# A prompt and sample decoder step on one core: sample attention dealt out inside the heads' loop, HBM tables cleared behind the cached values, first stage reordered

## What is computed

```python
def run_trunk(x, q_pos0, past_rows, past_win, ...):
    # layer 0: gMLP mixer, then dense SwiGLU (1024 -> 2816 -> 1024)
    z = gelu(rmsnorm(x) @ w_in);  u, v = split(z)
    v = layernorm(v, ln_g, ln_b)                       # the first stage of the kernel
    x = x + (u * (causal(W_s) @ v + b_s)) @ w_out
    x = x + swiglu(rmsnorm(x))
    # shared keys and values: compression, selection, window (4 groups of 64)
    kv = rmsnorm(x) @ w_kv                             # plus, for samples, cached pages and a window
    kc, vc = compress_blocks(...)                      # MLP over 32-row blocks, stride 16
    # layer 1: attention of 16 heads over three branches, ALiBi, sigmoid gates
    o = g0 * softmax(q kc) vc + g1 * softmax(q ks) vs + g2 * softmax(q kw) vw
    x = x + o @ w_out
    x = x + moe(rmsnorm(x))                            # top 2 of 8 SwiGLU experts
    return rmsnorm(x), kv rows, window, normed v
```

## Time and profile before

| | |
|---|---|
| Runs | 1326.03 us median, 1325.71 to 1331.93 |
| Profiled execution | 1325.86 us, its span 1324.3 us |
| TensorE busy | 1248.7 us (94%) |
| VectorE busy | 1042.1 us (79%) |
| ScalarE busy | 927.7 us (70%) |
| GpSimd busy | 76.4 us (6%) |
| Mean granted clock of TensorE | 0.977 of full speed |

### The profile page before, as it was taken

How to read it: one execution, slowest core, us unless ns; L and a number is a source line. 1 busy time by engine, 2 the same in 40 slices (tenths; PEclk the granted TensorE clock), 3 DMA queues, 4 the chain that set the end, 5 groups by cost and what they waited for, 6 DMA issues and landing times.

```text
span 1324.3 us, 21438 instructions
## 1 busy us (share of the span) xinstructions
PE 1248.7 (94%) x7272; PEld 1063.9 (80%) x7272; DVE 1042.1 (79%) x1463; ACT 927.7 (70%) x1378; POOL 76.4 (6%) x77
## 2 busy tenths in 40 slices
PE   6889999999996879999999999999999999999996
PEld 6879999999964668788788888888888888887874
DVE  6767666567523965898998998998998998989985
ACT  5555444456462895787987987987888888878863
POOL 1000000004210000200000000000000000003400
PEclk9999999999996889899999999999999999999998
DMA  8374455557589108699998998998998998998930
GB/s 342 129 252 172 183 191 192 191 191 254 160 318 418 61 4 347 266 423 393 357 416 333 388 413 322 406 406 319 413 402 324 415 392 333 416 380 326 410 133 33
DMA packets 59711, 391.50 MB, mean 296 GB/s; under 512 B 6686, under 2 KB 12962, under 8 KB 21186
## 3 DMA queue, kind: packets, MB, share of 16 engines
q1 hardware_dynamic: 51010, 354.29, 68.0%
q0 software_dynamic: 8640, 36.40, 7.4%
HBM read 367.41 MB, written 27.45 MB: 298 GB/s over the span
## 4 chain that ended last, share of the span: by engine, by line
PE 73%; DVE 10%; ACT 7%; issue 5%; SPq 3%; DMA 2%; DVEq 0%; ACTq 0%
PE bank L1838 16%; PE bank L1840 16%; PE bank L1839 16%; PE bank L1469 7%; PE bank L1470 7%; PE bank L1471 7%; DVE w_lo L1351 3%; ACT arena L756 2%; SPq L429 2%; DMA win_v_past<-in_win_v 2%; DVE d_lo L969 1%; PE bank L1823 1%; ACT slc_v L763 1%; ACT d_hi L604 1%; ACT w_hi L831 1%
## 5 line engine op out<-in xcount | busy, mean ns | idle before, releaser
L1351 DVE TENSOR_TENSOR w_lo<-raw,w_hi 128x1024 fp32r<-128x1024 f32 x528 | 622.7, 1218 | 36.0 <-ACT w_hi L831 18.4
L831 ACT CAST w_hi<-raw 128x1024 fp32r<-128x1024 f32 x528 | 543.2, 1056 | 93.3 <-PE bank L1840 92.3
L1838 PE MATMUL bank<-w_hi,xg_hi 128*128 128x512 f32 x704 | 275.0, 391 | 1.5 <-DVE w_lo L1351 1.5
L1840 PE MATMUL bank<-w_hi,xg_lo 128*128 128x512 f32 x704 | 274.4, 390 | 0.0
L1839 PE MATMUL bank<-w_lo,xg_hi 128*128 128x512 f32 x704 | 274.0, 389 | 0.0
L969 DVE TENSOR_TENSOR d_lo<-ring,d_hi 128x1024 fp32r<-128x1024 f32 x120 | 146.0, 1223 | 92.4 <-ACT d_hi L604 92.3
L1469 PE MATMUL bank<-hA_hi,d_hi 128*128 128x264 f32 x640 | 185.9, 291 | 18.4 <-DVE hA_lo L959 9.1
L1470 PE MATMUL bank<-hA_lo,d_hi 128*128 128x264 f32 x640 | 183.2, 286 | 0.0
L1471 PE MATMUL bank<-hA_hi,d_lo 128*128 128x264 f32 x640 | 182.9, 286 | 0.0
L604 ACT CAST d_hi<-ring 128x1024 fp32r<-128x1024 f32 x120 | 124.8, 1043 | 66.9 <-PE bank L1471 60.0
L1838 PEld LDWEIGHTS bank<-w_hi,xg_hi 128*128 128x128 f32 x704 | 132.1, 188 | 29.3 <-DVE w_lo L1351 2.2
(11 more groups left out here) (311 smaller groups left out, 1485.1 us busy)
## 6 DMA issues: line engine op xcount, KB each, us to landing
raw<-in_moe SPq DMA_DIRECT2D x264, 1024.0 KB, 6.7
ring<-in_wd SPq DMA_DIRECT2D x29, 2048.0 KB, 8.4
out_rows<-zeros POOLq DMA_DIRECT2D x1, 6656.0 KB, 60.3
slot_rows<-zeros POOLq DMA_DIRECT2D x1, 6144.0 KB, 30.3
out_rows<-yrow POOLq DMA_DIRECT2D x8, 512.0 KB, 7.0
xs<-slot_rows POOLq DMA_DIRECT2D x7, 512.0 KB, 3.6
arena<-in_cmp_pages POOLq DMA_DIRECT2D x16, 128.0 KB, 3.3
X2v<-in_cmp_pages POOLq DMA_DIRECT2D x16, 128.0 KB, 2.6
```

What stands on the lines that cost most here:

```text
L831: nc.scalar.copy(w_hi[:, i % NSPLIT, :], raw[:, u % NRAW, ITEM * (i % 2):ITEM * (i % 2) + ITEM])\
L1351: V.tensor_tensor(w_lo[:, i % NSPLIT, :], raw[:, (i // 2) % NRAW, ITEM * (i % 2):ITEM * (i % 2) + ITEM], w_hi[:, i % NSPLIT, :].bitcast(F3 ...
L1838: T.matmul(out, lhs_hi, hi, start=first, stop=False)
L1840: return T.matmul(out, lhs_lo, hi, start=False, stop=last)
```

## The change

1. **First stage.** ScalarE rounds, and VectorE makes the remainder of, one item more before each gelu and behind each scaling (`round_to("vu", c + 1)`, `rest_to("vu", k + 1)`). The u scalings and the items are spread over the layer norm at other places.
2. **Third transpose group.** It goes to the bank STAT, without the wait for VectorE's copy.
3. **Sample scores** go to STAT and MISC instead of B[0] to B[2]; their exponentials `Ss` and the turned weights `PTs` lie in `X2v`, no longer in a buffer of the heads' scores.
4. **Sample attention** is cut into blocks (`sample_max`, `sample_scale`, `sample_turned`, `sample_out` on VectorE; `sample_turn`, `sample_values`, `sample_sum` on TensorE) that stand between the blocks of pairs 0 to 3. `scores(0)` no longer waits for the sample maxima, and `scores(1)` no longer stands behind the value product.
5. **Clears.** GpSimd waits for all cached values (`past_v_in`) before it issues them.

```diff
@@ gpsimd
             pool.wait_ge(zeros_ready, 1)
+            pool.wait_ge(past_v_in, 16 * (NS * PAGES + 1))
             for rows in (slot_rows.rearrange("b p n -> (b p n)"), out_rows[0:NO_ROW, :].rearrange("r n -> (r n)")):
@@ scalar
             for c in range(KC):
-                round_to("vu", c)
+                round_to("vu", c + 1)
                 act.wait_ge(v_scaled, c + 1)
...
             for c in range(KC):
-                round_to("vu", KC + c)
+                round_to("vu", KC + c + 1)
...
             exp_head(0)
             exp_head(1)
+            exp_head(2)
+            exp_head(3)
             act.wait_ge(orow_done, 1)
             nc.scalar.copy(orow[:, :], MISC[:, :]).then_inc(orow_ready, 1)
-            exp_head(2)
-            exp_head(3)
@@ vector
             for k in range(KC):
-                rest_to("vu", k)
                 scaled(vT[:, k, :], "vu", k, v_scaled)
+                rest_to("vu", k + 1)
                 if k:
                     add_up(vT, k - 1, v_ready, k)
             add_up(vT, KC - 1, v_ready, KC)
-            rest_to("vu", 8)
+            u_scale(0)
+            rest_to("vu", 9)
             dve.wait_ge(mean_done, 2)
             settle(V.tensor_copy(mu[:, :], STAT[:, 0:NT]))
             for k in range(KC):
                 V.tensor_tensor(vT[:, k, :], vT[:, k, :], mu[:, :], ALU.subtract).then_inc(ctr_ready, 1)
-            u_scale(0)
-            u_scale(1)
-            for k in range(KC):
-                if k == 4:
-                    u_scale(2)
-                rest_to("vu", 9 + k // 4)
+                if k == 3:
+                    u_scale(1)
+                    rest_to("vu", 10)
+            for k in range(4):
+                add_up(hB, k, csq_ready, k + 1)
+            u_scale(2)
+            rest_to("vu", 11)
+            for k in range(4, KC):
                 add_up(hB, k, csq_ready, k + 1)
             u_scale(3)
-            rest_to("vu", 11)
+            rest_to("vu", 12)
             inv_std(ln_rstd)
             for k in range(KC):
-                if k == 5:
-                    rest_to("vu", 12)
+                if k == 3:
                     u_scale(4)
+                    rest_to("vu", 13)
...
-            rest_to("vu", 13)
-            u_scale(5)
-            u_scale(6)
-            u_scale(7)
+            for c in range(5, KC):
+                u_scale(c)
+                rest_to("vu", 9 + c)
...
+            sample_max()
             biased_max(0)
-
-            dve.wait_ge(spt_done, 1)
...
+            sample_scale()
             biased_max(1)
-            dve.wait_ge(so_done, 1)
...
+            sample_turned()
             scale(0)
             for p in range(NH // 2 - 1):
                 if p + 2 < NH // 2:
                     biased_max(p + 2)
                 scale(p + 1)
+                if p == 0:
+                    sample_out()
@@ tensor
             for t, (a, z) in enumerate([(0, P), (P, NP), (NP, NT)]):
-                if t == 2:
-                    pe.wait_ge(vp_ready, 1)
                 for j, c in enumerate((6, 7, 10, 11)):
-                    i = T.transpose((T0, T1)[t % 2][0:z - a, j * P:(j + 1) * P], kvT[:, c, a:z], ident)
+                    i = T.transpose((T0, T1, STAT)[t][0:z - a, j * P:(j + 1) * P], kvT[:, c, a:z], ident)
...
             def scores(p):
-                if p == 0:
-                    pe.wait_ge(ss_max, 1)
-                else:
+                if p:
                     pe.wait_ge(s_biased, 2 * p)
...
-                if p == 0:
+                if p == 1:
                     pe.wait_ge(so_ready, 1)
...
+            scores(0)
+            scores(1)
+            pe.wait_ge(cmp2_ready, 2)
+            sample_turn()
             for p in range(NH // 2):
                 if p + 2 < NH // 2:
                     scores(p + 2)
+                if p == 0:
+                    sample_values()
                 turn(2 * p)
                 if p:
                     weigh(p - 1)
+                else:
+                    sample_sum()
                 turn(2 * p + 1)
             weigh(NH // 2 - 1)
```

149 lines of the change are left out of this document (75 added, 74 removed).

## The result

The change made the kernel faster, by little more than half of what was forecast: 1311.99 us median against 1325.87 (runs of 1308.13 to 1315.57), 13.9 us less; ratio 0.9879, 95% interval 0.9855 to 0.9903 (the two medians alone give 0.9895). The forecast was 1299.9 with a range from 1292 to 1308. The profiled execution took 1308.13 us, the lowest of the four; its span is 1306.5 us, against 1324.3 before.

The account below looks back on a forecast made before the run. The chain was taken as mostly TensorE's, with slack at 25 to 81 and 373 to 440 us. First stage 6.5 plus attention 19.5 gave 26.0 us off 1325.9: 1299.9 us, range 1292 to 1308.

Parts of the forecast that it names:

- product 5 held: First stage: GpSimd holds VectorE's remainder of item 5, so product 5 starts at 29.3 us; gain there 0.4 us.
- the third bank: Third transpose group: idle 2.59 us and slow first compression product go, 3.8 us earlier; bound 2.8.
- the window values: Attention: cached window values, asked for at 397 us, land by 408 (10.6 us) instead of taking 20.93.
- The first term of the sum: First stage: gating starts at 74.3 us, 6.7 earlier, and later stages pass it on; taken as 6.5 us.
- The second: Attention: `exp_head(4)` and `exp_head(6)` start 19.0 to 20.2 us earlier, third bank's 3.8 included; taken as 19.5 us.
- The bound of 3.5: First stage: lower bound on its gain, 3.5 us, if the clock falls over the idle ahead of the second mean.
- turns head 0 near 418: Attention: TensorE takes up the value product at 411.6 us, needs some 5.6, then turns head 0 near 418.
- the clears' move: Clears behind the cached values: 12.8 MB done by 450 us, before the experts' load near 470; wait costs nothing.
- (b): Attention: loop starts with TensorE at 1.2 GHz, gain there only 13 to 15 us; total 1305.4 us; chance 0.12.
- (a): First stage gives only 1.5 us, idle returning ahead of the second mean, half clock behind it; total 1304.9; chance 0.12.
- (c): Attention: moving the clears does nothing, page issue sets the time, values land at 420; total 1306.4 us; chance 0.06.
- (d): Attention: clock stays low throughout, small matmuls between short waits; slower, 1340 us; chance 0.03.

Follow-up runs that it names:

- bank_only: The kernel before with only the third transpose group moved to a bank of its own: 1327.9 us, ratio 1.0000.
- first_fill: The kernel before with the first stage's reordering plus filler matmuls where TensorE idled in that stage: 1321.2 us, ratio 0.9958.
- before_fill: The kernel before, old order, with filler matmuls in its own first-stage TensorE idle times: 1327.2 us, ratio 1.0004.
- clears_late: The changed kernel with GpSimd's clears also waiting for the sample output: 1307.5 us, ratio 0.9855 to the kernel before.
- after_again: The changed kernel run once more, unaltered: 1314.0 us, ratio 0.9902 to the kernel before.
- after: The changed kernel, first measurement and profile: 1312.0 us, ratio 0.9879 to the kernel before.
- first_only: The kernel before with only the first stage's reordering: 1329.1 us, ratio 1.0004.
- sum_later: The changed kernel with the sample sum (TensorE) and sample output (VectorE) one pair later: 1313.2 us, ratio 0.9874 to the kernel before.
- after_fill: The changed kernel with filler matmuls before the second mean and behind the three token tiles' transposes: 1304.3 us, ratio 0.9811 to the kernel before.
- fill_tok: The changed kernel with filler matmuls only behind the token tiles' transposes: 1305.5 us, ratio 0.9840 to the kernel before.
- late_fill: The changed kernel with all first-stage filler matmuls and clears issued after the sample output: 1303.2 us, ratio 0.9811 to the kernel before.
- att_fill: The changed kernel with first-stage fillers, late clears, and fillers behind the scores of pairs 0 and 1: 1302.0 us, ratio 0.9796 to the kernel before.
- before: The kernel without the change: 1325.87 us median when first compared, 1326 to 1328 over the runs.

## Why the prediction was wrong

**Where it was right.** The walk through the first stage up to the second mean, to 0.8 us; product 5 held, in four executions of twelve; the third bank (3.8 us forecast, where its own rows give 2.8 + 0.9; 4.35 in `bank_only`, and 8.3 less the first stage's 3.95 at the last sample score); the window values; the clears' traffic hidden behind other work (DMA engines quiet from some 440 us). The first term of the sum is about what the order is worth when the clock stays up: 6.0 us (`first_fill` against `before_fill`) or 6.8 (against before), forecast 6.5. The second, 19.5, is harder to judge. `rest_only`, which has all of the change but the first stage, took 17.5 us less than before (1310.7 against 1328.2). `clears_late` came to 19.2 (122.6 less 103.4), but with one more edit, in one execution, and against a short one of before (see below).

**The step that failed** is in the first stage: "From there to the first gating operation took 6.36 us" and "without them some 5.2. So gating starts at 74.3", with "3.5 if the clock falls over the idle ahead of the mean" as the bound, and then "Every stage from there to 362 us is TensorE's and passes it on". These price the way from the first token tile's copy to gating, and from there on, at full clock. `after_again` shows what it cost. The copy came at 67.97, which with its 1.25 us earlier start is the forecast's 69.1. From there to the first gating operation it took 7.7 us instead of 5.2 (75.69), and from there to the first addition to x 17.2 us, where before it was 10.0 (81.01 to 91.04).
In the old order product 15 ran at half clock behind its 3.08 us of idle time, but it was 24 large matmuls close ahead of the transposes, and the clock was up again before these. In the new one all products are done when the transposes begin (67.49 in the first profile), and what follows is eight transposes, 2.36 us of waiting, eight more, 0.67, eight more, 0.71, then the small gating matmuls. I walked the VectorE side of this and never asked what TensorE does there. In all five profiled executions with this order and no fillers (`after`, `after_again`, `first_only`, `clears_late`, `sum_later`) the clock fell there; in four of them it stayed at 0.50 until 91 to 93 us, although TensorE was busy for 21.1 to 21.6 of 23 us. There the value transposes came at 373.6 to 374.5, so the term was -2 us or so instead of +6.5. The bound of 3.5 was too high by more than 5: I bounded the loss by the one drop I saw before, some 3 us long, and the new place had a longer one. Fillers show it by themselves: 8 to 10 us between `after_again` and `after_fill` or `fill_tok`.
The Trainium skill (TensorE: Matmul & The Clock Gate, A second HAM failure mode) tells of a kernel in which frequent short idles between groups of matmuls make the clock alternate. By it the prediction had a rival, placed in the attention; the trace agrees in that the clock fell behind such waits, but at the transposes of the first stage, and there it stayed down through 18.7 us of work without a pause (`after_again`).

**The attention** fell short by less: its part took 108.4 us in the first profile and 106.2 to 109.4 in the other kernels with the new attention, `clears_late` aside, forecast 103.1. Two steps failed. The walk went along VectorE's queue and left TensorE with "turns head 0 near 418". Behind that turn TensorE still had the sample sum, the turn of head 1 and the scores of pair 3. They took 6.6 us at full clock (417.33 to 423.9 in `clears_late`), which puts pair 3 at 424.6 where the walk had it at 422.3; in the first profile they took 8.2 (415.94 to 424.15), and VectorE waited 3.58 us for them. And the sum priced the clears' move at nothing ("GpSimd has nothing else to do before the scatter beyond 500. I cost the wait at nothing."). Their 12.8 MB were hidden, but their issue, 5 us of GpSimd from 399.27, was not: it lay on VectorE's operations in the middle of the interleaved blocks. The rows give 3.2 us for it in the first profile (1.52 less 0.17, and 2.65 less 0.81), 1.8 in `after_again` and 1.5 in `after_fill`; `clears_late` gave 3.6 us against `after_again`, with a clock that was higher too, and with fillers in both kernels the late clears gave 1.1 us of median, inside the noise. So the hold is shown, its worth in the total is, by an estimate from these rows, 1 to 3 us.
The Trainium skill (SBUF — State Buffer, Who interferes with whom) lists VectorE's copies and operations with a scalar operand among those that can contend with GpSimd for a shared pair of ports, and says that whoever issues first gets it. The trace agrees: TENSOR_SCALAR took 1.52 and 2.65 us beside the issue, while reductions and TENSOR_TENSOR kept their times there (0.21 at 399.74, 0.16 at 401.55).
The rest is rival (b) in part: TensorE was granted 0.50 from 399 to 411, when the one queue held scores, value product and sample sum. The 24 matmuls of a pair's scores took 2.03 us at full clock (393.75), and 3.79 and 2.79 for pairs 2 and 3: 2.5 us on the way to `exp_head(6)` from these two alone. With the clears late as well, the attention took 103.4 us in one execution (`clears_late`, clock 0.95 from 399 to 411) and 108.0 in another (`late_fill`, 0.63), so the clock is worth up to 4.6 us there, the same size as the shortfall. That it is the clock alone is argued from these two executions, not shown by a run that held it up: in the one profile of `att_fill` the fall only moved.
One thing more stood behind the numbers. In the four other kernels that kept the old attention and the early clears it took 125.1 to 127.7 us (`first_only`, `first_fill`, `before_fill`, `bank_only`), so the profile of before, with 122.6, was a short one, as its 1325.9 us stands to the 1328 of later medians. Against 125 to 128 the changed attention (107.0 to 109.4 in `after`, `after_again` and `rest_only`) won 16 to 21 us, around the forecast's 19.5; the medians say 17.5. So of the 12 us that the total missed, the first stage has some 8.5 (-2 instead of 6.5) and the attention some 2; what is left is within the spread of the runs.

**The chances.** Faster at 0.96 was right. The forecast had 0.62, and (a) and (b), 0.12 each, were taken to exclude each other; both happened in part, (a) at another place and by a stronger fall of the clock than its own. A range built from rivals taken one at a time had no place for that. (c) fell with the window values' 9.2 us, and the slower case (d), a low clock through all of attention, didn't come: from 423 to 459 the clock was 1.00 in the first profile.

## What to carry to other kernels

When an edit pulls large matmuls away from in front of small ones that wait, price TensorE's clock over everything behind, not over the gap: here some 6 us of real gain disappeared into 20 us at half clock, and 3.6 us of useless matmuls in idle time (2.39, 0.61 and 0.61 in `after_fill`) brought it back. When blocks are dealt out in a loop, walk every engine's queue to the end of the stretch, not only that of the engine that seems to lead. Where a wait is moved so that GpSimd issues large transfers, look at what VectorE does in these microseconds, not only at the transfers. And profile a changed kernel more than once before its stages are compared: here one profile showed the first stage 4 us ahead, the next one 2 us behind.

## What the runs showed of the hardware

The granted clock stayed at 0.50, the lower level of 1.2 GHz, for over 20 us with TensorE at work for 21.61 of 23 us (`after_again`), on transposes, gating matmuls and the first product behind them; in another execution of the same kernel it was back after 3.4 us (71.4 to 74.8). A wait of 3.1 us ahead of product 15 was followed by the low clock in `before` and not in `rest_only`. In `late_fill` it fell at 387 us although TensorE's busy time was 1.00 in every microsecond from 381 to 394. GpSimd's issue of two clears held VectorE's TENSOR_SCALAR operations until it was over, and left reductions and TENSOR_TENSOR alone. Where VectorE's remainder and GpSimd's operation on operands in SBUF started together, either could be the one held: 3.44 us instead of 1.22, or 3.47 instead of 2.4.
